# Expert gate and residual moved into the PSUM sums of a mixture-of-experts layer, on one core

## The reference, cut to what matters

```
shift1, scale1, gate1, shift2, scale2, gate2 = adaln(cond, w_ada[i], b_ada[i])   # one row of 1024 each
x = LN(alpha * x + gate1 * mixer(x * (1 + scale1) + shift1))
x = LN(alpha * x + gate2 * hier_moe(x * (1 + scale2) + shift2))

def hier_moe(h):            # top-1 of 4 groups, then top-2 of its 8 experts
    ...
    for each block of tokens with one expert e:
        hb = silu(xb @ w_gate[e]) * (xb @ w_up[e])
        out = (hb @ w_down[e]) * w          # w: each token's routing weight
        y[token] += out
```

## Time and profile before

| | |
|---|---|
| three runs | 1358.57 us median (1357.22 to 1359.48) |
| the profiled execution | 1363.88 us; its span, first to last instruction, 1362.0 us |
| TensorE matmul busy, share of the span | 1134.6 us, 83% |
| TensorE weight load | 609.9 us, 45% |
| VectorE | 466.9 us, 34% |
| ScalarE, GpSimd | 153.5 us and 156.6 us, 11% each |
| HBM traffic | 281 GB/s over the span, some 415 GB/s where the weights stream |
| mean granted TensorE clock | 0.898 of full |

### The profile page before, as it was taken

The page is one execution under the profiler, slowest core; times in us unless marked ns, Lnnn a source line. Parts: engine busy times, 40 slices in busy tenths (PEclk is TensorE's granted clock), DMA queues, the critical chain, the costliest instruction groups (busy, mean ns, idle before and its releaser), DMA issues.

```text
span 1362.0 us, 29280 instructions
## 1 busy us (share of the span) xinstructions
PE 1134.6 (83%) x11192; PEld 609.9 (45%) x11193; DVE 466.9 (34%) x1238; ACT 153.5 (11%) x406; POOL 156.6 (11%) x304
## 2 busy tenths in 40 slices
PE   5899998789599999767664999887965999999761
PEld 1333335535355555434332444444443555555430
DVE  0120207767622222211117002277674322222117
ACT  0110115600000000000002000355000000000000
POOL 2000001301011111111000210000001211111100
PEclk9899997989699999978776999979966999999876
DMA  9866794026987999999984998200259999997991
GB/s 368 296 275 245 298 352 188 1 62 227 390 335 311 414 415 414 414 415 415 416 326 185 133 136 177 78 0 12 67 194 407 410 412 378 414 394 312 412 399 46
DMA packets 79899, 379.35 MB, mean 279 GB/s; under 512 B 14728, under 2 KB 15184, under 8 KB 52200
## 3 DMA queue, kind: packets, MB, share of 16 engines
q1 hardware_dynamic: 61504, 343.48, 65.1%
q0 software_dynamic: 12272, 32.52, 8.9%
q10 hardware_dynamic: 6072, 2.69, 0.7%
HBM read 375.49 MB, written 7.87 MB: 281 GB/s over the span
## 4 chain that ended last, share of the span: by engine, by line
PE 45%; DMA 32%; issue 10%; DVE 8%; ACT 2%; DVEq 2%; POOLq 1%; SPq 0%; POOL 0%; ACTq 0%; PEldq 0%
DMA ring<-in_w_up_dram 25%; PE ps L796 16%; PE ps L1083 7%; PE ps L948 6%; DMA ring<-in_w_down_dram 5%; PE ps L1096 4%; PE ps L1066 3%; DMA ring<-in_w_ada_dram 2%; PE ps L772 1%; PE ps L1053 1%; POOLq L461 1%; DVEq L1126 1%; PE ps L893 1%; PE ps L881 1%; PE ps L915 1%
## 5 line engine op out<-in xcount | busy, mean ns | idle before, releaser
L1083 PE MATMUL ps<-ring,xs 128*32 128x256 f32 x4672 | 293.3, 404 | 69.0 <-DMA ring<-in_w_up_dram 68.8
L796 PE MATMUL ps<-ring,hT 128*128 128x512 f32 x576 | 255.8, 604 | 8.0 <-ACT hT L631 4.2
L1083 PEld LDWEIGHTS ps<-ring,xs 128*32 128x32 f32 x4672 | 161.4, 115 | 186.6 <-issue 99.4
L796 PEld LDWEIGHTS ps<-ring,hT 128*128 128x128 f32 x576 | 109.9, 193 | 152.9 <-issue 142.7
L1096 PE MATMUL ps<-ring,hm 128*32 128x256 f32 x2336 | 142.2, 382 | 3.8 <-DMA ring<-in_w_down_dram 3.8
L1600 DVE TENSOR_TENSOR hp<-sg,ps 128x128 f32<-128x128 f32 x73 | 21.0, 288 | 321.1 <-ACT sg L735 321.1
L1066 PE MATMUL ps<-yo,place 32*128 32x256 f32 x1800 | 127.0, 413 | 1.9 <-DVE place L1608 1.9
L1066 PEld LDWEIGHTS ps<-yo,place 32*128 32x128 f32 x1800 | 85.9, 197 | 47.6 <-issue 34.0
L1096 PEld LDWEIGHTS ps<-ring,hm 128*32 128x32 f32 x2336 | 67.9, 109 | 67.4 <-DVE hm L1601 19.6
L735 ACT ACTIVATE sg<-ps 128x128 f32<-128x128 f32 x73 | 20.3, 278 | 604.6 <-PE ps L1083 604.6
L948 PE MATMUL ps<-ring,qT 128*128 128x512 f32 x192 | 86.3, 611 | 2.0 <-DVE qT L1382 1.6
(11 more groups left out here) (293 smaller groups left out, 841.7 us busy)
## 6 DMA issues: line engine op xcount, KB each, us to landing
ring<-in_w_gate_dram SPq DMA_DIRECT2D x82, 1024.0 KB, 15.0
ring<-in_w_up_dram SPq DMA_DIRECT2D x82, 1024.0 KB, 15.3
ring<-in_w_down_dram SPq DMA_DIRECT2D x82, 1024.0 KB, 15.5
ring<-in_w_ada_dram SPq DMA_DIRECT2D x48, 1024.0 KB, 8.0
ring<-in_w_qkv_a_dram SPq DMA_DIRECT2D x12, 1024.0 KB, 5.2
ring<-in_w_qkv_b_dram SPq DMA_DIRECT2D x12, 1024.0 KB, 14.9
modb<-mdram POOLq DMA_DIRECT2D x12, 512.0 KB, 7.9
ring<-in_w_o_a_dram SPq DMA_DIRECT2D x4, 1024.0 KB, 11.1
```

The lines of the kernel that those rows point to most:

```text
L796: ins = mm(ps[:, 2 * t + hf, :], lhs[:, k, t * P:(t + 1) * P], raw[:, slot, kk * D + hf * 512:kk * D + (hf + 1) * 512], start=(k == 0), st ...
L1083: ins = mm(ps[j * BLK:(j + 1) * BLK, 6, 0:W].rearrange("p (a f n) -> p a f n", a=2, f=G), xs[:, k, :], w[:, :, kk * DE:(kk + 1) * DE].rear ...
```

## The change

Four things change, all around the experts.

1. **The gate goes into each block.** The gate rows, cut in four pieces of 256 columns and laid out as the blocks' results are, are loaded to `gt` by eight small DMAs in place of two of full rows (`load_gate_pieces`). VectorE divides them by alpha once, in block 0. `take_y` no longer copies 128x256 values out of bank 7 but multiplies them by both rows of `gt`, giving 128x512 values; `add_block` takes the half that belongs to the tile.
2. **The residual goes into the sums.** For tiles 0 and 1, four matmuls of the identity with `x` take the place of four of the six zero matmuls. Tile 2's `x` is not ready then: banks 4 and 5 are still cleared, and two identity matmuls add it between the two loops. The sums then hold x + gate * experts / alpha, the layer norm's argument over alpha, so epsilon becomes EPS / ALPHA ** 2.
3. **The statistics are read from PSUM.** `take_sums` and `take_experts` are gone. `measure` runs the statistics on the banks (four pieces of 256 for tiles 0 and 1, two of 512 for tile 2), and ScalarE, VectorE and `finish` read PSUM in place of `x`. In layer 0 TensorE waits for both normalised tiles before it transposes the first, and half of tile 1's `take_h` goes from ScalarE to VectorE. In layer 1 all three tiles share one `spread`, and the three `finish` stand at the end.
4. **Order in the routing.** The matmuls that fill banks 0 to 5 go ahead of the tables, and the weight list's matmuls follow them. The token tables and the clearing of `yo`, `xg` and `place` go ahead of `fold`, to the end of the attention. Six small operations that build the weight matrices become one of 128x342.

```diff
@@ POOL
-                load_gates(l, 1)
+                load_gate_pieces(l)
                 load_affine(l, 0, modb)
+            def load_gate_pieces(l):
+                for cnd in range(2):
+                    for j in range(G):
+                        pool.dma_start(gt[j * BLK:(j + 1) * BLK, cnd, :],
+                                       mdram[l, cnd:cnd + 1, 5 * D + j * WD:5 * D + (j + 1) * WD].to_broadcast([BLK, WD]))\
+                            .then_inc(gt_ld, 16)
@@ ACT, layer 0's tail
-                        act.activation(x[:, t, :], x[:, t, :], ACT.Identity, bias=nmr[:, t:t + 1], scale=rstd[:, t:t + 1])\
+                        act.activation(x[:, t, :].rearrange("p (j w) -> p j w", j=G), acc_tile(t), ACT.Identity,
+                                       bias=nmr[:, t:t + 1], scale=rstd[:, t:t + 1])\
@@ PE, layer 1's start
+                    pe.wait_ge(h_rdy[l], 2)
                     transpose_tiles(lambda t: x[:, t, :], h_rdy[l], hT_ps[l], by_run, range(2))
@@ PE, between the slot list and the experts
+                pe.wait_ge(yo_rdy[l], 1)
+                pe.sem_inc(y_added[l], 1)
+                pe.wait_ge(mod_used, l + 1)
+                for j in range(G):
+                    mm(ps[:, j, :].rearrange("p (t w) -> p t w", t=2), ident, x[:, 0:2, j * WD:(j + 1) * WD],
+                       start=True, stop=False)
+                for bank in range(G, 2 * NT):
+                    mm(ps[:, bank, :], place[:, 0:P], cst[:, 0:512], start=True, stop=False)
+                pe.wait_ge(rt_dve[l], 11)
                 for i in range(2 * NT):
                     ... (the weight list, now to bank 7 ahead of the tables)
                 pe.wait_ge(tab_rdy, l + 1)
-                pe.wait_ge(tok_rdy, l + 1)
...
-                pe.wait_ge(yo_rdy[l], 1)
-                pe.sem_inc(y_added[l], 1)
-                for bank in range(2 * NT):
-                    mm(ps[:, bank, :], place[:, 0:P], cst[:, 0:512], start=True, stop=False)
@@ PE, between the loops of three and of two
+                pe.wait_ge(x2_done, l + 1)
+                done = table(pe, n_trip * BUFS + (T_CUM + 1), 3, NB + LEAST - 2)
+                wait_apart(pe, pe_steps, y_added[l], done + 1)
+                for bank in range(G, 2 * NT):
+                    ins = mm(ps[:, bank, :], ident, x[:, 2, (bank - G) * 512:(bank - G + 1) * 512], start=False, stop=False)
+                ins.then_inc(x2_added, 1)
+                pe.wait_ge(x2_added, l + 1)
@@ DVE
-                    v.tensor_copy(yo[:, :], ps[:, 7, 0:WD])
+                    v.tensor_tensor(yo[:, :, :], ps[:, 7, 0:WD].unsqueeze(1).to_broadcast([P, 2, WD]), gt[:, :, :], ALU.mult)
-                for i in range(2 * NT):
-                    v.tensor_scalar(col(3200 + i * NBX, NBX), iota[:, 0:NBX], sf[:, i:i + 1],
-                                    gatew[:, i % 2, i // 2:i // 2 + 1], ALU.is_equal, ALU.mult).then_inc(rt_dve[l], 1)
+                v.scalar_tensor_tensor(a_slot, a_slot, 0.0, col(1700, 2 * NT).unsqueeze(2).to_broadcast([P, 2 * NT, NBX]),
+                                       ALU.is_gt, ALU.mult).then_inc(rt_dve[l], 1)
-            def take_sums(l, t):
-            def take_experts(l, t):
+            def measure(t):
+                parts = [ps[:, j, t * WD:(t + 1) * WD] for j in range(G)] if t < 2 else [ps[:, G + i, :] for i in range(2)]
+                for i, part in enumerate(parts):
+                    v.bn_stats(st[:, i, :], part)
```

More of the change, by code:

```diff
@@ L1383, in _ @@
                                         subc[:, :].unsqueeze(2).to_broadcast([P, KD, P]), ALU.mult).then_inc(oT_rdy[l], 1)
+                for t in range(NT):
+                    v.tensor_scalar(tokens[:, t * P:(t + 1) * P], cst[:, C_IOTA:C_IOTA + P], float(t * P), None, ALU.add)
+                v.memset(yo[:, :, :], 0.0)
+                v.memset(xg[:, :, :], 0.0)
+                v.memset(place[:, :], 0.0)
+                dve.drain()
+                dve.sem_inc(yo_rdy[l], 1)
                 fold(l, 0)
@@ L1613, in body @@
                     take_x(b + 1, (lane + 1) % lanes, turn + (lane + 1) // lanes)
+                    if isinstance(b, int) and b == 0:
+                        dve.wait_ge(gt_ld, 32 * G * (l + 1))
+                        chain(v.tensor_scalar(gt[:, :, :], gt[:, :, :], 1.0 / ALPHA, None, ALU.mult))
                     take_y(b)
@@ L1663, in _ @@
                 else:
[L1664 to L1670 removed]
+                    measure(2)
+                    spread(l, 0, 3)
+                    dve.wait_ge(lnb_ld, 256)
+                    for t in range(NT):
+                        finish(t)
 _INS = ['x_prompt', 'x_sample', 'cache_a_k', 'cache_a_v', 'cache_b_k', 'cache_b_v', 'c', 'c_ctx', 'w_ada', 'b_ada',
```

130 lines of the change are left out of this document (56 added, 74 removed).

## The result

The changed kernel takes 1338.5 us (median of 4 runs, 1335.6 to 1339.8) against 1358.6 us (1357.2 to 1359.5): ratio 0.984, 95% interval 0.983 to 0.986, some 20 us less. Repeated later, the same kernel took 1338.4 (5 runs, 1336.9 to 1340.4), ratio 0.985, interval 0.984 to 0.986. The time is inside the forecast range and 5 us above the 1333.5 forecast. The profiled execution took 1335.58 us, its span is 1333.8.

What follows compares the result with a forecast made beforehand. Bound: TensorE's projections and attention; layer 0's experts by buffers coming free, then weight loads; VectorE behind the experts. 9.5 + 0.5 + 5.2 + 9.8 = 25.0 us off 1363.88 gives 1338.9, for the median 1333.5; range 1325 to 1343.

Steps and rivals of the forecast that it cites:

- the two tails: Behind each layer's experts: fewer VectorE passes and statistics from PSUM gain 5.2 us in layer 0, 9.8 in layer 1.
- the last product: At the end of each layer nothing covers take_y's product, which replaces a copy: a cost of 0.27 us.
- Layer 0's start: Block 0 of layer 0's experts starts earlier, reaching the stage's end: 9.5 us gained, bounds 5.2 and 11.5.
- layer 1's is not: Layer 1's experts start 10 us earlier, but against the weight stream: 0.5 us gained, bounds -1.5 and +2.5.
- the product: In take_y, 0.69 us for a copy's 0.42, beside the next block's gate_up: cost 0 in the blocks.
- the group: Added TensorE work between the expert loops, about 2.8 us: cost 0, bounds 0 and 2.8 a layer; exposed, chance 0.10.
- The tail in layer 0: From layer 0's last expert sum to the projections, which start at 734.0, not 739.22: 5.2 us, bounds 4.4 and 5.8.
- its queue 0.6 us: Behind layer 0's experts, ScalarE's queue adds some 0.6 us before the projections start.
- 6.2 us from the last sum to ScalarE: Sign expected in the changed profile behind layer 0's experts: ScalarE starts 6.2 us after the last sum.
- The clock term: TensorE stands still about 2.6 us before block 0, so the clock falls: 1.6 us off the start's gain.
- the 1.6 for the clears: Token tables and three clears leave VectorE's routing in layer 0: 1.6 us gained, bounds 0 and 2.1.
- The slower rival: take_y's product outlasts its cover: from 2.9 us each of 73 blocks pays the excess; at 3.3, 1363; chance 0.02.

Runs made afterwards that it cites:

- the late fill: Changed kernel with the filling of the banks put back behind the tables and the weight list, in layer 0 alone: 1342.9 us.
- the same edit there: Changed kernel with the banks filled behind the tables and the weight list in layer 1 alone: 1336.6 us.
- three products: Changed kernel with take_y's product made three times in place of once in each block: 1342.2 us.
- two groups: Changed kernel with two more 512-column matmuls that add zeros beside the two identity matmuls between the loops, in both layers: 1336.2 us.
- the kernel with three zero matmuls: Changed kernel with three more 128x128x512 matmuls that add zeros, behind the weight list, in both layers: 1334.4 us.
- the one without the group: Changed kernel without the two identity matmuls between the loops in layer 1 alone: 1335.8 us.

## Why the prediction was right, and where its sum was off

Stages of the four unaltered traces in us, before (two), after (two), and the term foreseen:

| stretch | before | after | gain | foreseen |
|---|---|---|---|---|
| to layer 0's last modulated row | 335.7, 334.5 | 334.4, 334.3 | 0.8 | 0 |
| from it to expert 4's issue | 91.2, 90.5 | 82.2, 81.5 | 9.1 | 9.5 |
| to layer 0's last up weights | 278.8, 278.8 | 278.6, 278.6 | 0.2 | 0 |
| to the end of its last sum | 10.7, 8.5 | 8.7, 8.8 | 0.8 | -0.3 |
| to the projections | 22.7, 22.4 | 17.1, 17.1 | 5.4 | 5.5 |
| to layer 1's first load | 269.9, 269.1 | 270.7, 270.8 | -1.3 | 0 |
| to its last up weights | 314.4, 314.6 | 313.5, 313.5 | 1.0 | 0.5 |
| to the end of its last sum | 9.2, 8.5 | 8.8, 10.9 | -1.0 | -0.3 |
| to the last `finish` | 26.4, 26.4 | 16.6, 16.6 | 9.8 | 10.1 |

(The 9.8 and the 5.2 foreseen for the two tails are both net of 0.3 for the last product, which lies one stretch earlier here: the prediction has it in layer 0 as the start of the statistics at 717.5 and not 717.23.)

**What held.** Layer 0's start is set by when buffers come free and pays (9.1 for 9.5; the late fill shows it for 6 of them), layer 1's is not (shown by the same edit there), the product and the group are hidden (shown by three products, by two groups and by none), and the two tails cost what was foreseen. The tail in layer 0 went step by step: ScalarE 6.28 us after the first statistics step (6.25 foreseen), the transposes 2.40 us after ScalarE's start (2.4), and the projections 7.72 us behind the transposes' start (7.85 foreseen). What stands in between is not what the prediction says: the 16 records of tiles 0 and 1 are over after 3.64 us (3.65), at 716.97, tile 2 is ready at 716.13, so its transposes follow at once and end after 4.62 us in all, and from there the projections wait 3.10 us for ScalarE. Its sixteen pieces of `hT` run without a pause from 715.30 to 720.99 and set the end; the prediction gave its queue 0.6 us. That the sum came out is in part luck. The sign "6.2 us from the last sum to ScalarE" was read from the first statistics step, which starts 0.74 us behind the last sum: from the sum it is 7.02.

**Layer 0's start in its parts.** Its two steps were off in opposite directions. Counted from the last modulated row, block 0 started 36.4 us after it, foreseen 36.9 (372.6 - 335.74), before 47.9: 11.5 us and not 11.1. The clock rose at 362 us, 5.4 us after the token list's start where 6.9 were foreseen, so the weight list ended 32.9 us after the row (34.3 foreseen); the rest behind it was 3.45 us and not 2.6. The clock term was 1.6 and measured 2.5 (6.10 us against 3.6): the added matmuls that fill the rest take exactly that back. And the 1.6 for the clears depends on the clock: "the matmuls that step waits for are over by then" is true of the trace that I read. In the second trace of before those matmuls ran at low clock and ended together with the clears, so there the clears hid them. From the last modulated row to that step it was 19.2 and 19.1 us in the two traces of before, 17.5 and 16.7 in those of after, but 19.3 in the kernel with three zero matmuls and in the one without the group, which have no clears either and met the low clock. In such an execution the removal brings nothing.

**The slower rival's rule.** "From a product of 2.9 us on, each of 73 blocks pays the excess" was wrong in two ways. A product of some 2.2 us was hidden; at 3.75 us (2.99 + 0.69 and the pause) a block took 1.16 us longer, so the point lies near 2.6 (an estimate from these two), the hand-over between the engines not being in the 2.9. And only about half of the excess is paid. The 3.3 us at which it would have met the time before is nearly five plain products of 0.69, not four. None of this touched the forecast.

**Where 4 to 5 us of the sum went.** The gains of the four traces add up to 24.8, the forecast's sum was 25.0, but the medians lie only 20.1 to 20.8 apart. That the first two agree so well is partly luck: four stretches went another way than foreseen (0.8 and 0.8 us gained, 1.3 and 1.0 lost) and nearly cancel. The step that was off is the last: "so 1338.9; it stands 5.3 above the median, so for the median 1333.5". It carries the terms of one execution over to the median of all, as if each term were the same in every execution. Two things speak against that. The term for the clears is 1.7 to 2.4 us at one clock and nothing at the other. And the two traces of after are the fastest of nine executions of their kernel (1335.6 and 1336.9, the others 1337.1 to 1340.4), while the first of before was slower than any other of its kernel (1363.9): the four traces make the gain look some 4 us larger than the runs do. What the other executions of the changed kernel spend more is likely where the clock falls in some and not in others. The eleven traces of the changed kernel and of its variants with the same tokens show how much that can be: the routing up to the token list took 21.4 to 24.1 us, projections and attention behind layer 0's experts 267.2 to 271.1, and, where the product was left alone, the last block of each layer 8.7 to 10.9. Each spread is 2 to 4 us in code that is the same. No trace shows a long execution of the unaltered changed kernel, so this stays argued, not shown, and a term of some -4 us stays open.

**The range.** The sum of the bounds, 1329 to 1342, leaves out the bound of 2.8 us a layer that the prediction gives the group between the loops; with it the upper end is 1347. The measured 1338.5 lies inside either way.

## What to carry to other kernels

Work that waits only for old data belongs ahead of the late step, not behind it, but whether that pays is set by what frees the next buffer: here the same edit was worth 6 us in one layer and nothing in the other, and the DMA share while TensorE worked through the first experts told them apart (0.14 between 395 and 400 us in layer 0; in layer 1 of the same trace it is 1.01 to 1.03 in every 5 us from 1050 to 1100). Look for what a deleted instruction was hiding, and read that from more than one execution, since the clock decides how long the hidden work is. A rest in front of a long stretch of matmuls costs more than its own length; matmuls that add zeros in it brought the next free buffer 2.5 us nearer.

## What the runs showed of the hardware that was not expected

- Two levels of the granted clock in the same code. In layer 0's routing the 32 records of 512 columns at L779 (L772 before) took 5.1 to 5.8 us in some executions, with a pause of 0.8 to 1.5 us behind them and small matmuls at full clock after it (0.85 us for six of 32 columns), and 3.64 us in others, with a pause of 4.0 to 4.2 us and the same small matmuls at 1.46 to 1.49 us. The two went together in all fourteen traces, fast records and slow small matmuls in three of them. It looks as if running fast first made it slow after, by the longer rest; no run here fills that rest, so this is not shown. The changed kernel's second trace, and under it that of the kernel with three zero matmuls:

```profile
340.12 5.70 PE L779 MATMUL ps<-ring,cond 128*32 128x512 f32 x32
346.72 0.35 PE L1008 MATMUL ps<-cst,kT 128*32 128x1 f32 x6 [0.90 <-DVE kT L1481]
...
347.19 0.86 PE L1015 MATMUL ps<-kT,cst 128*128 128x32 f32 x6
```

```profile
339.05 3.64 PE L779 MATMUL ps<-ring,cond 128*32 128x512 f32 x32
346.88 0.35 PE L1008 MATMUL ps<-cst,kT 128*32 128x1 f32 x6 [4.19 <-DVE kT L1483]
...
347.43 1.49 PE L1015 MATMUL ps<-kT,cst 128*128 128x32 f32 x6
```
- Layer 0's and layer 1's last half blocks took 1.93 us in some traces and 2.7 to 3.64 in others (1.93 and 3.64 in layer 1 of the changed kernel's two), and four added matmuls in the rests of the last loop kept the three half blocks ahead of the last at full clock, but not the last (2.99 and 3.53 us).
- VectorE's statistics over 1024 PSUM columns cost 1.42 us in four pieces and 1.30 in two, no more than from SBUF (685 ns for 512). A step with one tensor operand took 1.34 us from PSUM for 1024 columns where it took 0.81 from SBUF. That agrees with the Trainium skill, VectorE: DVE Perf Modes, section "Mode 2×_2P — use both read ports for one tensor", by which the double rate of such a step needs its source in SBUF, because PSUM has only one read port. It cost nothing here, because tile 2 waited for TensorE.
